# A decoder layer with gathered experts: ScalarE scales the third and fourth tile's convolution taps, and TensorE sums them earlier

## The chip, the cores and the metric

The kernel runs on one core of one Trainium2 chip. A core has five engines with instruction streams of their own: TensorE (PE in the profile; its weight loads are PEld), VectorE (DVE), ScalarE (ACT), GpSimd (POOL) and SyncE (SP). They meet only at semaphores. Each executes its stream in order, so an instruction that waits holds up everything behind it on its engine. The metric is the device time of one launch in microseconds; before the change it is 2165.56 us, the median of three runs.

## The reference, cut to what matters

One decoder layer is computed for a prompt of 512 tokens, in four tiles of 128, and for 32 sample tokens. Each tile has a front part (projections, causal depthwise convolution, attention over keys that an indexer selects, merge, norm) and an expert part, in which each token reads 128 rows of a table u and 128 rows of a table v, chosen by top-k.

```python
def conformer_conv(u, prev, conv_w, conv_b, ...):      # CONV_W = 31, D_CONV = 512
    full = jnp.concatenate([prev, u], axis=1)
    y = lax.conv_general_dilated(full, conv_w[:, None, :], ..., feature_group_count=D_CONV) + conv_b
    y = jax.nn.silu(layer_norm(y, conv_ln_g, conv_ln_b))
    ...

def attn_prompt(q, k, v, qi, ki, wi):                  # per block of 128 queries
    idx, valid = select_keys(indexer_scores(qib, wib, ki), pb, topk)      # topk = 128
    return sparse_attend(qb, _gather_rows(k, idx), _gather_rows(v, idx), valid)

def peer_ffn(x2, ...):
    u = peer_u[eidx]; v = peer_v[eidx]                 # 128 rows each for a token
    a = jax.nn.gelu(jnp.einsum('nd,nhed->nhe', x2, u), approximate=False)
    return jnp.einsum('nhe,nhed->nd', (g * a), v)
```

Per channel the convolution is a sum over 31 shifts ("taps") of the gated tokens, each scaled by one weight of the channel.

## The kernel before, in words

The prompt's tiles are counted t = 0 to 3. "Third tile" is t = 2 and "fourth tile" t = 3. Their fronts run while the expert part of the tile ahead (t = 1, t = 2) is under way on the same engines.

**Expert part.** GpSimd issues 544 gathers of u rows and 544 of v rows (line 884), each of 128 rows of 1,024 floats, into a ring of 11 places of the buffer `rings`. A u gather is used up by one "dot" of VectorE (line 2177, 128x1024). Two v gathers are used up by one "expert pair" of TensorE (line 1780, eight traced matmuls of 128x512), for which ScalarE copies a small column of weights (line 1262, 128x4) for each two pairs. A gather into a place waits until the row that lay there has been used (lines 877 to 880), so GpSimd can be at most a ring ahead of VectorE and TensorE.

**Front of the third and fourth tile.** After the load and the rotation, TensorE transposes the parts, ScalarE copies them to SBUF (line 987, the convolution's input `uT3` last). Then come, in this order: the index phase (for each of eight heads a product of TensorE, line 1526, a Relu of ScalarE, line 1132, and a weighted sum of VectorE into `score`, line 2076); the top-k of 16 rounds on VectorE (lines 1844 and 1847), in which the front needs neither TensorE nor ScalarE; and the attention of 16 heads (VectorE line 2037, ScalarE lines 1067 and 1082, TensorE lines 1613, 1596 and 1627).

**The taps.** Within the first part of the attention VectorE makes for each of the 31 taps one product of the shifted tokens with the tap's weights (`scaled_taps`, line 2022, 128x512), and TensorE adds it into the upper half of the bank `wide` by a matmul with the identity (`added_taps`, line 1513). Two buffers take turns: `stage_1`, and `score`, which is free once the top-k is over. So scaling tap k waits for the sum of tap k - 2, and the sum of tap k waits for its scaling. After tap 31 ScalarE moves the sum out of the bank (`convolved`, line 1018). The attention needs the bank's upper half only from its ninth head on (line 1621).

**What sets the order.** Each engine's stream is put together by a merge of generators (`run`, `merge`, lines 619 to 630). Each generator yields planned times before its pieces, and the piece with the least time is put next. A front's times are fractions (`AT_IDX` = 0.05, `AT_TOPK` = 0.09, `AT_ATT` = 0.20, `AT_TAIL` = 0.48) that `CLOCK_T` turns into planned microseconds for the third and fourth tile. `tap_at` gives the taps' times. The plan decides only the order in each stream; at run time semaphores decide.

## Time and profile before

| | |
|---|---|
| runs | 2162.22, 2165.56, 2166.86 us; median 2165.56 us |
| profiled execution | 2169.81 us; span of its instructions 2168.0 us |
| busy, share of the span | TensorE 66%, weight loads 25%, VectorE 62%, ScalarE 13%, GpSimd 56% |
| granted TensorE clock, mean | 0.823 |
| DMA, mean over the span | 315 GB/s |

The span is what lies between the first and the last instruction, and the shares are means over stages that differ much. Four stages concern the change. In the third tile's front the index phase runs from about 740 to 757 us, the top-k to 800 us, the taps to 855 us beside the attention's first heads, and the rest of the attention to 892 us. In the fourth tile's front these are 1136, 1152, 1195, 1259 and 1306 us. In the rows below an instruction stands with its line, its engine and the names of what it writes and reads; "idle before <-releaser" is how long its engine had waited for it and what ended that wait. A tap's matmul is traced as two instructions (x2), an expert pair as eight (x8).

### The profile page before, as it was taken

How to read it: one execution, taken by the hardware profiler on the slowest of the kernel's cores; microseconds unless marked ns; L12 is line 12 of the kernel's file. 1: busy time of each engine (PE TensorE's matmuls, PEld its weight loads, DVE VectorE, ACT ScalarE, POOL GpSimd, SP SyncE). 2: the span in 40 equal slices, each digit the busy share in tenths (PEclk: the TensorE clock that was granted, in tenths of full speed). 3: DMA queues.
4: the chain of work that ended last, by engine and by line, in shares of the span. 5: the costliest groups of instructions: out<-in, count | busy, mean ns of one | idle time of the engine just before them, and what ended most of it. 6: DMA issues, size and time to landing. Idle time of an engine off the chain costs nothing.

```text
span 2168.0 us, 18693 instructions
## 1 busy us (share of the span) xinstructions
PE 1435.1 (66%) x5765; PEld 541.4 (25%) x5765; DVE 1342.3 (62%) x3160; ACT 273.3 (13%) x667; POOL 1216.8 (56%) x1107
## 2 busy tenths in 40 slices
PE   7889999488964518776655887855533347566335
PEld 3444444232220104322111342311100012122001
DVE  4318965991159599947939876587569974103441
ACT  1411111112000202201010121200000002000000
POOL 1003454665555655856867567677656565346654
PEclk9999999799998859589676988887666567779878
DMA  8717999878888977989999789999989979979996
GB/s 303 315 63 258 324 366 373 300 242 312 301 309 307 389 254 251 340 277 331 332 387 351 236 316 352 351 355 336 373 277 397 360 258 362 354 282 336 375 348 245
DMA packets 207454, 682.68 MB, mean 315 GB/s; under 512 B 26901, under 2 KB 54933, under 8 KB 200787
## 3 DMA queue, kind: packets, MB, share of 16 engines
q0 software_dynamic: 157376, 581.67, 74.3%
q1 hardware_dynamic: 42971, 90.66, 11.6%
q10 hardware_dynamic: 7008, 9.17, 1.2%
q8 instruction: 46, 0.75, 0.1%
q14 instruction: 53, 0.43, 0.1%
HBM read 668.88 MB, written 12.94 MB: 314 GB/s over the span
## 4 chain that ended last, share of the span: by engine, by line
PE 34%; DVE 24%; issue 12%; POOL 11%; DMA 8%; SPq 5%; another core or an unknown queue 3%; ACT 2%; POOLq 0%; ACTq 0%; DVEq 0%
POOL rings L884 11%; DVE rings L2177 9%; PE acc L1780 7%; PE acc L1349 6%; DMA rings<-peer_v,late 4%; PE wide L1349 3%; PE wide L1374 3%; DVE small L1844 2%; PE bank L1487 2%; PE wide L1513 2%; SPq L740 2%; PE acc L1316 2%; DMA rings<-peer_u,late 2%; SPq L748 2%
## 5 line engine op out<-in xcount | busy, mean ns | idle before, releaser
L884 POOL DMA_INDIRECT rings<-peer_u,late x544 | 621.3, 1142 | 487.4 <-DVE late L2177 193.5
L1780 PE MATMUL acc<-rings,z_stages 128*32 128x512 f32 x2048 | 564.2, 711 | 426.9 <-issue 232.4
L884 POOL DMA_INDIRECT rings<-peer_v,late x544 | 587.0, 1079 | 362.3 <-PE acc L1780 160.3
L2177 DVE CUSTOM_DVE_ANT_0 rings<-rings,uah 128x1024 f32<-128x1024 f32 x288 | 347.3, 1223 | 150.4 <-DMA rings<-peer_u,late 142.6
L2177 DVE CUSTOM_DVE_ANT_0 rings<-rings,late 128x1024 f32<-128x1024 f32 x256 | 308.9, 1223 | 86.7 <-DMA rings<-peer_u,late 71.0
L1780 PEld LDWEIGHTS acc<-rings,z_stages 128*32 128x32 f32 x2048 | 120.6, 121 | 817.3 <-issue 811.5
L1349 PE MATMUL acc<-rings 128*128 128x512 f32 (+1 forms) x352 | 147.1, 569 | 0.1
L1513 PE MATMUL wide<-z_stages,ident_s 128*128 128x512 f32 x96 | 56.7, 675 | 90.9 <-DVE z_stages L2022 90.6
L1262 ACT COPY z_stages<-late 128x4 f32<-128x4 f32 x136 | 26.1, 199 | 547.3 <-PE acc L1780 416.0
L1349 PEld LDWEIGHTS acc<-rings 128*128 128x128 f32 x352 | 62.6, 190 | 70.1 <-issue 69.3
L1316 PE MATMUL acc<-rings 128*128 128x512 f32 (+2 forms) x176 | 70.1, 546 | 14.2 <-DMA small<-quarter 12.4
L1349 PE MATMUL wide<-rings,uah 128*128 128x512 f32 (+1 forms) x176 | 74.3, 565 | 1.3 <-DVE late L1894 1.3
L1941 DVE MAX8 uah<-zt 128x8 f32<-128x128 f32 x68 | 19.4, 285 | 84.5 <-ACT zt L1050 68.0
L1627 PE MATMUL wide<-keep,soft_score 128*128 128x64 f32 x320 | 50.2, 305 | 21.7 <-ACT soft_score L1082 17.8
L1374 PE MATMUL wide<-w_out_s,uah 128*128 128x512 f32 x128 | 63.5, 644 | 1.4 <-ACT uah L1028 1.4
L1067 ACT ACTIVATE soft_score<-soft_score,small 128x128 f32<-128x128 f32 (+3 forms) x64 | 35.7, 558 | 213.1 <-DVE small L2042 213.0
L1487 PE MATMUL bank<-w_query_s,uah 128*128 128x512 f32 x128 | 61.2, 620 | 1.4 <-ACT uah L1035 1.4
L1627 PEld LDWEIGHTS wide<-keep,soft_score 128*128 128x128 f32 x320 | 46.9, 218 | 49.4 <-ACT soft_score L1082 31.0
L1513 PE MATMUL wide<-soft_score,ident_s 128*128 128x512 f32 x90 | 51.6, 657 | 5.0 <-DVE soft_score L2022 5.0
L1596 PE MATMUL bank<-keep,queries 64*128 64x128 f32 (+3 forms) x128 | 48.4, 526 | 4.7 <-issue 4.7
L1513 PEld LDWEIGHTS wide<-z_stages,ident_s 128*128 128x128 f32 x96 | 16.6, 203 | 119.4 <-issue 96.5
L2177 DVE DVE_READ_ACCUMULATOR2_ANT late<- 128x1 f32 x544 | 44.7, 82 | 0.0
(296 smaller groups left out, 1592.9 us busy)
## 6 DMA issues: line engine op xcount, KB each, us to landing
rings<-w_in SPq DMA_DIRECT2D x36, 1024.0 KB, 7.1
rings<-peer_u,late POOLq DMA_INDIRECT x544
rings<-peer_v,late POOLq DMA_INDIRECT x544
z_rows<-z_stages ACTq DMA_DIRECT2D x30, 256.0 KB
soft_score<-ln SPq DMA_DIRECT2D x6, 1024.0 KB, 7.7
zt<-z_rows SPq DMA_DIRECT2D x2, 2596.0 KB
w_out_s<-w_out POOLq DMA_DIRECT2D x1, 4096.0 KB, 17.1
w_query_s<-w_query POOLq DMA_DIRECT2D x1, 4096.0 KB, 14.0
```

What stands on the lines that cost most here:

```text
L740: return sp.value_load(page_s[0:1, at:at + 1], min_val=0, max_val=N_POOL - 1)
L748: sp.dma_start(smp_ki[r][k // 2][rows, j * PAGE:(j + 1) * PAGE], io["kidx_T"][pages[j]]).then_inc(kidx_in[r], 16)
L884: nc.gpsimd.indirect_dma_start(ring[:, place, :], None, table, offs).then_inc(row_in[place], 16)
L1316: last = nc.tensor.matmul(acc[:, i % 2 * BLK + lo:i % 2 * BLK + hi], xT_0[:, k, :], w[:, c, :], start=(k == 0), stop=(k == KC - 1))
L1349: last = nc.tensor.matmul(z_bank[j][:, 0:width], x[j][:, m, :], w[:, c, :], **flags)
L1374: last = nc.tensor.matmul(dst[0:n, half * BLK:(half + 1) * BLK], lhs[:, c, 0:n], rhs[:, c, half * BLK:(half + 1) * BLK], start=(c == 0), s ...
L1487: last = nc.tensor.matmul(s_bank[r][0:n, :], aT3[:, c, 0:n], wqu[:, c, r * BLK:(r + 1) * BLK], start=(c == 0), stop=(c == KC - 1))
L1513: nc.tensor.matmul(wide[:, BLK:], ident[:, :], scaled_of[k % 2].rearrange("p c n -> p (c n)"), start=(k == 0), stop=(k == CONV_W - 1), ski ...
L1596: last = nc.tensor.matmul(s_bank[g % 2][:, k * seen:(k + 1) * seen], qT3[half_rows[h % 2], h // 2, :], kT3[half_rows[h % 2], h // (N_HEADS ...
L1627: last = nc.tensor.matmul(wide[:, o * HEAD_DIM:(o + 1) * HEAD_DIM], pt2[:, g % 2, at * P:(at + 1) * P], v3[:, j, kv * HEAD_DIM:(kv + 1) * ...
L1780: last = nc.tensor.matmul(acc_v[QUAD * j:QUAD * (j + 1), half * BLK:(half + 1) * BLK], lone[:, quad % LONE, j, QUAD - 1 - m:2 * QUAD - 1 - m],
L2177: V.tensor_tensor_reduce(out=ring[:, place, :], in0=ring[:, place, :], in1=h, scale=1.0, scalar=0.0, op0=ALU.mult, op1=ALU.add, accum_out= ...
```

## The change

For the third and fourth tile the scaling of the taps goes from VectorE to ScalarE: each tap is four activations (`Copy` with the tap's weight as a scale for each partition), one for each group of 128 channels, where VectorE made one product of 128x512. The taps' planned times go from fractions 0.204 to 0.33 to 0.047 to 0.21, that is from the attention's first part to the time from the transposes to the attention; TensorE's sums follow at +0.008. Since `score` is in use then, the second buffer is another part of `zt` (the gates of the convolution's input, used up by then). The second tile keeps VectorE, its buffers and its times; only the move out of the bank gets a planned time that is 0.007 later.

```diff
-    scaled_of = (stage_1.rearrange("p (c n) -> p c n", c=CC), score.rearrange("p (c n) -> p c n", c=CC))
+    by_channels = lambda x: x.rearrange("p (c n) -> p c n", c=CC)
+    scaled_1 = (by_channels(stage_1), by_channels(score))
+    scaled_later = (by_channels(stage_1), by_channels(zt[:, Z_B:Z_B + D_CONV]))
...
-    def tap_at(k):
+    def tap_at(t, k):
 
-        return AT_ATT + 0.004 + 0.126 * k / CONV_W
+        return AT_ATT + 0.004 + 0.126 * k / CONV_W if t == 1 else 0.047 + 0.163 * k / CONV_W
+
+    def scaled_of(t, k):
+
+        return (scaled_1 if t == 1 else scaled_later)[k % 2]
...
@@ ScalarE @@
+        def scaled_taps(t):
+
+            for k in range(CONV_W):
+                yield tap_at(t, k)
+                if k == 0:
+                    act.wait_ge(t_copied, groups_before(t) + GROUPS)
+                if taps_before(t) + k >= 2:
+                    act.wait_ge(tap_added, taps_before(t) + k - 1)
+                for c in range(CC):
+                    last = nc.scalar.activation(scaled_of(t, k)[:, c, :], uT3[:, c, k:k + P], ACT.Copy,
+                                                scale=cp[:, c, k:k + 1])
+                last.then_inc(tap_scaled, 1)
...
-                yield from merge(itertools.chain(rectified(t), attention(t, AT_ATT, AT_TAIL)), convolved(t))
+                yield from merge(itertools.chain(rectified(t), attention(t, AT_ATT, AT_TAIL)),
+                                 itertools.chain(scaled_taps(t) if t >= 2 else iter(()), convolved(t)))
...
@@ TensorE, added_taps @@
-                yield tap_at(k) + 0.003
+                yield tap_at(t, k) + (0.003 if t == 1 else 0.008)
...
@@ VectorE @@
-                yield from merge(attention(t, AT_ATT, AT_TAIL), scaled_taps(t))
+                yield from merge(attention(t, AT_ATT, AT_TAIL), scaled_taps(t) if t == 1 else iter(()))
```

What this does to the streams is seen at three places. The changed kernel's lines lie 20 further down in the parts of TensorE and VectorE (2177 becomes 2197, 1780 becomes 1800, 1513 becomes 1533).

VectorE, the start of the third tile's attention; L2022 is a scaled tap, L2177 a dot, L2037 with L2042 one head of the attention. Before:

```order
L2022 TENSOR_TENSOR z_stages<-uah,conv_p 128x512
L2177 ISA rings,late<-rings,uah 128x1024
L2177 ISA late 128x1
L2022 TENSOR_TENSOR soft_score<-uah,conv_p 128x512
L2037 ISA soft_score,small<-bank,soft_score 128x384
L2037 ISA small 128x1
L2042 TENSOR_SCALAR small<-small 128x1
L2022 TENSOR_TENSOR z_stages<-uah,conv_p 128x512
L2177 ISA rings,late<-rings,uah 128x1024
L2177 ISA late 128x1
L2022 TENSOR_TENSOR soft_score<-uah,conv_p 128x512
```

And now (L2197 is the dot, L2057 with L2062 the head):

```order
L2197 ISA rings,late<-rings,uah 128x1024
L2197 ISA late 128x1
L2057 ISA soft_score,small<-bank,soft_score 128x384
L2057 ISA small 128x1
L2062 TENSOR_SCALAR small<-small 128x1
L2197 ISA rings,late<-rings,uah 128x1024
L2197 ISA late 128x1
```

The 31 taps are gone from between the dots; the order of the dots and the heads is the same.

ScalarE, the fourth tile's index phase; L1132 is a head's Relu, L943 the copy of the values ahead of it. Before:

```order
L1112 COPY uah<-uah 128x4x30
L987 COPY uah<-bank 128x4x128
L943 COPY keep<-zt 128x256
L1132 ACTIVATE soft_score<-bank 128x512 x5
L1262 COPY z_stages<-late 128x4
L1132 ACTIVATE soft_score<-bank 128x512 x3
```

And now (L1152 is the Relu, L1027 a tap's four pieces):

```order
L949 COPY keep<-zt 128x256
L1027 ACTIVATE z_stages<-uah,conv_p 128x128 x4
L1152 ACTIVATE soft_score<-bank 128x512
L1027 ACTIVATE zt<-uah,conv_p 128x128 x4
L1152 ACTIVATE soft_score<-bank 128x512
L1027 ACTIVATE z_stages<-uah,conv_p 128x128 x4
L1152 ACTIVATE soft_score<-bank 128x512
L1027 ACTIVATE zt<-uah,conv_p 128x128 x4
L1152 ACTIVATE soft_score<-bank 128x512
L1027 ACTIVATE z_stages<-uah,conv_p 128x128 x4
```

A tap stands ahead of each Relu, the first one too.

TensorE, from the fourth tile's index products (L1526) over its first two score products (L1596) to the attention; L1780 are expert pairs, four for a pair, L1513 is a tap. Before:

```order
L1526 MATMUL bank<-keep,queries 128x512 x3
L1780 MATMUL acc<-rings,z_stages 32x512 x4
L1526 MATMUL bank<-keep,queries 128x512 x5
L1780 MATMUL acc<-rings,z_stages 32x512 x4
L1596 MATMUL bank<-keep,queries 128x512 x2
L1780 MATMUL acc<-rings,z_stages 32x512 x20
L1513 MATMUL wide<-z_stages,ident_s 128x512
L1513 MATMUL wide<-soft_score,ident_s 128x512
```

And now (L1546 index product, L1533 tap, L1800 expert pair):

```order
L1546 MATMUL bank<-keep,queries 128x512 x2
L1533 MATMUL wide<-z_stages,ident_s 128x512
L1546 MATMUL bank<-keep,queries 128x512
L1533 MATMUL wide<-zt,ident_s 128x512
L1800 MATMUL acc<-rings,z_stages 32x512 x4
L1546 MATMUL bank<-keep,queries 128x512
L1533 MATMUL wide<-z_stages,ident_s 128x512
L1546 MATMUL bank<-keep,queries 128x512
L1533 MATMUL wide<-zt,ident_s 128x512
L1546 MATMUL bank<-keep,queries 128x512
L1533 MATMUL wide<-z_stages,ident_s 128x512
L1546 MATMUL bank<-keep,queries 128x512
```

Six taps stand ahead of the last index product, the rest between the expert pairs of the top-k, four or five taps to a pair; the attention's heads have none.

## Rows read from the trace of the kernel before

**Rows 1.** The stages' view: busy us of each engine (instructions), granted clock, DMA share, GB/s

```profile
744.00:757.00 13.00, 7.70 (x30) 2.09 (x26) 7.15 (x13) 3.63 (x6) 9.58 (x10) 0.91 1.03 409
757.00:801.00 44.00, 0.00 (x0) 0.00 (x0) 42.83 (x93) 0.00 (x0) 21.76 (x20) 0.50 0.81 267
801.00:856.00 55.00, 46.07 (x144) 20.88 (x144) 54.52 (x111) 10.04 (x28) 30.55 (x26) 0.92 0.76 238
856.00:935.00 79.00, 57.36 (x155) 31.10 (x154) 71.13 (x134) 14.52 (x35) 65.23 (x46) 0.65 0.89 317
1136.00:1152.00 16.00, 13.15 (x32) 3.12 (x32) 15.15 (x23) 4.71 (x10) 12.76 (x11) 0.79 0.86 293
1152.00:1195.00 43.00, 17.46 (x40) 3.20 (x40) 41.84 (x83) 1.48 (x2) 30.12 (x28) 0.68 0.98 367
1195.00:1265.00 70.00, 61.94 (x219) 27.59 (x220) 57.34 (x113) 14.47 (x36) 41.90 (x33) 0.93 0.73 246
```

**Rows 2.** The chain of waits by line, 757 to 935 us

```profile
by line: POOL rings L884 31.6%; DVE rings L2177 29.0%; issue 12.2%; DVE soft_score L1847 5.3%; DVE small L1844 4.3%; DVE z_stages L2022 4.3%; DVE soft_score L2022 4.3%; DMA rings<-peer_u,late 3.6%; DVE soft_score L2037 2.2%; PE wide L1513 1
```

**Rows 3.** Waits of GpSimd, 801 to 856 us: total us, times, longest

```profile
POOL rings L884 <- DVE late L2177: 22.6, 21, 2.4
```

**Rows 4.** Timeline of GpSimd: start us, us, operation [idle before <-releaser]

```profile
801.25 0.94 POOL L884 DMA_INDIRECT rings<-peer_u,late  x1 [2.45 <-DVE late L2177]
...
856.06 1.68 POOL L884 DMA_INDIRECT rings<-peer_u,late  x1 [0.87 <-DVE late L2177]
...
887.99 0.95 POOL L884 DMA_INDIRECT rings<-peer_u,late  x1 [0.30 <-issue]
...
932.26 1.98 POOL L884 DMA_INDIRECT rings<-peer_u,late  x1 [0.30 <-issue]
```

**Rows 5.** Timeline of VectorE, third tile's first scaled tap and the dot behind it

```profile
805.00 0.69 DVE L2022 TENSOR_TENSOR z_stages<-uah,conv_p 128x512 f32<-128x512 f32 x1
805.60 1.22 DVE L2177 CUSTOM_DVE_ANT_0 rings<-rings,uah 128x1024 f32<-128x1024 f32 x1
```

**Rows 6.** The chain of waits by line, 1195 to 1265 us

```profile
by line: PE wide L1513 39.1%; PE acc L1780 13.1%; PE bank L1596 11.4%; DVE rings L2177 10.0%; PE wide L1627 6.4%; PE bank L1613 5.4%; DVE soft_score L2037 3.7%; issue 3.6%; DVE z_stages L2022 2.7%; ACT queries L1018 1.3%; ACT soft_score L10
```

**Rows 7.** Waits of GpSimd, 1195 to 1265 us

```profile
POOL rings L884 <- PE acc L1780: 19.7, 5, 6.4
```

**Rows 8.** Timeline of GpSimd, fourth tile's taps

```profile
1195.22 1.68 POOL L884 DMA_INDIRECT rings<-peer_v,late  x1 [2.51 <-DVE late L2177]
...
1206.44 1.63 POOL L884 DMA_INDIRECT rings<-peer_u,late  x1 [0.30 <-issue]
1214.51 0.94 POOL L884 DMA_INDIRECT rings<-peer_u,late  x1 [6.44 <-PE acc L1780]
...
1264.23 0.94 POOL L884 DMA_INDIRECT rings<-peer_u,late  x1 [2.47 <-PE acc L1780]
```

**Rows 9.** Timeline of TensorE: index product, expert pair, taps, expert pair

```profile
1136.51 1.12 PE L1526 MATMUL bank<-keep,queries 64*128 64x512 f32 x2 [0.79 <-ACT soft_score L1132]
...
1188.71 3.34 PE L1780 MATMUL acc<-rings,z_stages 128*32 128x512 f32 x8 [4.07 <-DMA rings<-peer_v,late]
1199.94 2.04 PE L1513 MATMUL wide<-z_stages,ident_s 128*128 128x512 f32 x2 [7.88 <-DVE z_stages L2022]
...
1212.33 1.91 PE L1780 MATMUL acc<-rings,z_stages 128*32 128x512 f32 x8
```

**Rows 10.** The chain of waits in order of time: start us, us, what

```profile
1222.93 1.91 PE wide L1513 x4
```

**Rows 11.** ScalarE's groups by form, from SBUF with a pointer bias

```profile
L1067 ACT ACTIVATE soft_score<-soft_score,small 128x128 f32<-128x128 f32 x16 | 6.2, 390 | 4.0 <-DVE small L2042 4.0
```

**Rows 12.** The chain of waits in order of time, a gather's landing

```profile
928.25 6.39 DMA rings<-peer_u,late
```

**Rows 13.** Timeline of VectorE, fourth tile's index sums

```profile
1136.57 0.75 DVE L2076 SCALAR_TENSOR_TENSOR soft_score<-soft_score,small,conv_acc 128x512 f32<-128x512 f32 x1 [5.57 <-ACT soft_score L1132]
...
1148.17 1.56 DVE L2076 SCALAR_TENSOR_TENSOR soft_score<-soft_score,small 128x512 f32<-128x512 f32 x2
```

More of the change, by code:

```diff
@@ L1010, in conv @@
             last.then_inc(conv_act, 1)
+        def scaled_taps(t):
[9 more added lines that the diff above has]
+                last.then_inc(tap_scaled, 1)
         def convolved(t):
-            yield tap_at(CONV_W) + 0.005
+            yield tap_at(t, CONV_W) + 0.012
             act.wait_ge(tap_added, taps_before(t + 1))
@@ L1512, in added_taps @@
                 pe.wait_ge(tap_scaled, taps_before(t) + k + 1)
-                nc.tensor.matmul(wide[:, BLK:], ident[:, :], scaled_of[k % 2].rearrange("p c n -> p (c n)"),
+                nc.tensor.matmul(wide[:, BLK:], ident[:, :], scaled_of(t, k).rearrange("p c n -> p (c n)"),
                                  start=(k == 0), stop=(k == CONV_W - 1), skip_group_check=True).then_inc(tap_added, 1)
@@ L2014, in scaled_taps @@
             for k in range(CONV_W):
-                yield tap_at(k)
+                yield tap_at(t, k)
                 if k == 0:
@@ L2021, in scaled_taps @@
                     dve.wait_ge(tap_added, taps_before(t) + k - 1)
-                V.tensor_tensor(scaled_of[k % 2], uT3[:, :, k:k + P], cp[:, :, k:k + 1].to_broadcast([P, CC, P]),
+                V.tensor_tensor(scaled_of(t, k), uT3[:, :, k:k + P], cp[:, :, k:k + 1].to_broadcast([P, CC, P]),
                                 ALU.mult).then_inc(tap_scaled, 1)
```

## The prediction, made before the changed kernel ran

> **What bounds the kernel now.** I read the stages' view first, then the chain of waits in the two stretches that the change touches, then what GpSimd waits for there, and last the timelines of single instructions. The gathers are the bulk of the work, and where they slow down is where the kernel loses time. The stages' view shows two such stretches, and they are the two in which the taps lie: 801 to 856 us moves 238 GB/s and 1195 to 1265 us moves 246 GB/s, against 317 GB/s and 367 GB/s in the stretches beside them [rows 1].
>
> In the third tile VectorE is the limit. It is busy 54.52 of 55 us [rows 1], the chain from 757 to 935 us runs over VectorE's dots and taps first and over GpSimd's issues behind them [rows 2], and GpSimd waits 22.6 us for dots [rows 3]. From 856.06 us on GpSimd waits for nothing but its own issue. The timeline of GpSimd, read through, has 27 intervals between gathers from 801.25 to 856.06 us (one record is missing), 17 to 887.99 us and 27 to 932.26 us [rows 4]: 2.03, 1.88 and 1.64 us each. The middle pace belongs to a VectorE that eats up the landed rows without a pause, the last one to a VectorE that waits for rows.
>
> In the fourth tile the limit is TensorE. Its taps hold 39.1% of the chain from 1195 to 1265 us [rows 6], it is busy 61.94 of 70 us [rows 1], and GpSimd waits 19.7 us for expert pairs that stand behind taps [rows 7]: the gather after 1206.44 us starts at 1214.51 us, when the pair of 1212.33 us has run [rows 8, 9]. There are 32 intervals from 1195.22 to 1264.23 us, 2.16 us each.
>
> **What the change takes away, third tile.** VectorE loses 31 taps. One is 0.69 us long but takes 0.60 us of the stream (805.00 to 805.60 us) [rows 5], so 31 x 0.60 = 18.8 us, all in a stretch where VectorE is full. Behind it stands GpSimd, which can't give all of that back. Without taps VectorE still has a stock of landed rows, which took from 856 to 888 us to run down; so I let 18 gathers go at 1.88 us and the other 53 of the 71 at 1.64 us: 34 + 87 = 121 us where 131.0 us stand now [rows 4]. That is -10 us. The bounds are 0 (all 71 at 1.88 us would be 133 us) and -18.8 us (all of VectorE's time comes back).
>
> **Fourth tile.** TensorE's 31 taps leave the stretch; a tap takes 0.96 us of it at the high clock (x4, two taps, 1.91 us) [rows 10], 29.6 us in all. The 32 gathers then go at 1.64 us: 52.5 instead of 69.0 us [rows 8], -16.5 us. Bounds: at 1.88 us it is 60 us, -9 us; at the rate of the top-k before it, 367 GB/s for 246 x 70 = 17.2 MB [rows 1], it is 47 us, -22 us.
>
> **What it adds: ScalarE.** The trace has no scaling from SBUF by a pointer in pieces of 128. The nearest row is an Exp from SBUF with a pointer bias, 390 ns [rows 11]. Four pieces take 1.56 us without overlap and 1.29 us with the 0.09 us by which VectorE's tap and the dot behind it overlap [rows 5]; with an overlap of 0.15 us, my lower bound, it is 1.1 us. I take 1.25 us, 39 us for a tile. From 1136 to 1195 us ScalarE is busy 4.71 + 1.48 us of 59 [rows 1], so this fits. What it costs is order. A tap stands ahead of the first Relu of the index phase, and behind that Relu are the sum on VectorE, the top-k and the dots in the same stream: +1.3 us in each tile.
>
> The Trainium skill has a rule that speaks against this part. "VectorE: DVE Perf Modes", section on the TRN2 errata, says that a ScalarE or VectorE instruction which reads SBUF pays a fixed extra latency each time, so that one wide operation is cheaper than four narrow ones; "ScalarE: Activation LUTs", What ACT_TABLE_LOAD costs, gives 186 ns + 0.833 ns an element, 93 ns more for a pointer and 93 ns of overlap, from which I estimate 1.27 us for the four pieces against VectorE's one at 0.60 us. By it ScalarE spends twice what VectorE saves, and the sum stays, since ScalarE has the room. The 390 ns of a 128-wide piece agree with it.
>
> **What it adds: TensorE in the index phase and the top-k.** From the third tile's index phase to its attention TensorE is idle 5.3 of 13 us and then 44 of 44 us [rows 1], so its taps are covered; I add 1 us for the taps between the index products, 2.3 with the tap ahead, say +2 us. In the fourth tile six taps (5.8 us) stand ahead of the last index product, and TensorE had 16 - 13.15 = 2.9 us idle there [rows 1]: +3 us, with the tap ahead +4 us. The sums of VectorE that wait for it took from 1136.57 to 1149.7 us [rows 13]. Bounds: 0, and all 5.8 us at the low clock with its tap twice as long, +12 us.
>
> From there to 1195 us TensorE has to fit eight index products and two score products at 1.1 us (the pair of rows of one is 1.12 us), seven expert pairs at 1.9 us and 31 taps at 0.96 us [rows 9, 10]: 11 + 13 + 30 = 54 of 59 us. It fits, at the high clock only, and pairs that wait for a row hold the taps behind them. The streams show four or five taps between two pairs. I take +3 us for pairs that come late at the end of the top-k. Tap 31 on ScalarE stands behind the first Exp of the attention, which waits for the end of the top-k; TensorE's sum of it stands ahead of the first head's transposes: +1 us for both tiles.
>
> **The sum.** -10 - 16.5 + 2 + 4 + 3 + 1 = -16.5 us. Nothing later is tied to an absolute time: the fourth tile's front starts when the third tile is routed, the sample's when the fourth is. Against the profiled execution (2169.81 us, its span 2168.0 us and 1.8 us around it) that is 2153.3 us. The runs' median is 4.2 us under the profiled execution, so I predict 2149 us for the median.
>
> **Rivals.**
> - *Both stretches free up wholly.* VectorE's 18.8 us and GpSimd's 19.7 us of waits [rows 7] both come back and the additions are 6 us: -32 us, 2133 us. For it: in the top-k of the fourth tile the DMA reaches 367 GB/s beside a VectorE busy 41.84 of 43 us [rows 1], so gathers can go faster than my 1.64 us. Against it: 1.88 us with VectorE full of dots [rows 4].
> - *GpSimd is the limit anyway.* The gathers keep 1.88 us while VectorE is dense: third tile 0, fourth tile -9 us, additions +10 us: 2166 us, no change. For it: issues of up to 1.98 us with no wait [rows 4].
> - *TensorE runs the taps at the low clock, slower.* The place is the fourth tile from the index phase to the top-k's end. In it the granted clock was 0.79 and 0.68, and in the third tile's top-k 0.50 [rows 1]; a tap's two rows at 1199.94 us, after an idle time of 7.88 us, took 2.04 us, and a pair 3.34 us against 1.91 us [rows 9]. At the low level (1.2 GHz) 31 x 1.9 + 7 x 3.3 + 10 x 2.2 = 104 us have to go into 59 us; if half the time is low, the last pairs come some 20 us late, and a ring of 11 gathers at 1.5 us (28 in 43 us of the top-k), less 6.4 us of landing [rows 1, 12], covers about 10 us. It decides once TensorE falls behind by more than that. Then the fourth tile's gain turns into waits of GpSimd in the top-k: -10 + 2 - 16.5 + 12 + 22 = +9.5 us, 2175 us. Against it: in the fourth tile's taps, with TensorE almost full, the granted clock was 0.93 [rows 1], and here it would be as full. The Trainium skill states the ground of both, in "TensorE: Matmul & The Clock Gate", section on the HAM clock gate: the clock is throttled by default and activity releases it. The rows at 1199.94 us and 1222.93 us agree.
> - *The taps are scaled by ScalarE but still end in the attention*, since the two buffers tie ScalarE to TensorE and TensorE waits for rows. Then TensorE keeps part of its taps behind 1195 us; half of the fourth tile's gain goes: 2157 us. It lies within the forecast's own range.
>
> **How the numbers follow.** Forecast, with its smaller relatives (2141 to 2159 us): 0.50. Both stretches free: 0.16. GpSimd the limit: 0.18. Low clock: 0.16. A measurement of this kernel can tell about 0.2%, 4.3 us, from no change. Faster by more than that: 0.48 of the forecast, 0.16, and 0.04 of GpSimd's case, 0.68. Within it: 0.02, 0.12 and 0.02, 0.16. Slower: 0.02 and 0.14, 0.16. The range goes from the free case's lower side to just above no change, 2130 to 2170 us; it leaves out most of the low clock's case.
>
> **What would show it.** VectorE from the end of the third tile's top-k: heads of the attention and dots with nothing between them, and soon waits for landed rows. GpSimd's waits for dots (22.6 us) and for pairs (19.7 us) shrink to a few us. The 71 and 32 intervals average 1.7 us. ScalarE's 124 pieces for a tile at about 0.39 us. The index phase 2 and 4 us longer. The prediction is wrong if the fourth tile's top-k stretch falls under 340 GB/s with GpSimd waiting for pairs in it, or if GpSimd's intervals stay at 1.9 us without a wait.

## The result, and the profile after

The changed kernel took 2141.7 us (median of 9 runs, 2136.9 to 2159.6), the kernel before beside it 2168.6 us (9 runs). The ratio is 0.9884, 95% interval 0.9843 to 0.9924: faster by 16 to 34 us. Predicted were 2149 us, 2130 to 2170. The profiled execution's span is 2139.7 us, 28.3 us under the one before.

The stages' view after, for the third tile's index phase, top-k and attention, then the same of the fourth:

```profile
core 0: us, PE busy (x) PEld busy (x) DVE busy (x) ACT busy (x) POOL busy (x), PEclk, DMA share, GB/s
741.00:760.00 19.00, 17.25 (x43) 4.99 (x44) 7.94 (x14) 11.25 (x36) 7.87 (x10) 0.91 0.89 326
760.00:803.00 43.00, 26.27 (x50) 7.03 (x48) 41.90 (x89) 28.22 (x89) 22.03 (x21) 0.89 0.78 248
803.00:885.00 82.00, 59.89 (x178) 36.88 (x178) 73.38 (x156) 20.75 (x57) 65.32 (x46) 0.50 0.84 285
1124.00:1140.00 16.00, 15.92 (x40) 4.30 (x40) 12.88 (x20) 12.60 (x37) 10.05 (x9) 1.00 0.94 335
1140.00:1183.00 43.00, 36.32 (x90) 9.84 (x88) 41.87 (x82) 27.78 (x91) 28.84 (x28) 0.92 0.86 317
1183.00:1286.00 103.00, 76.67 (x313) 35.69 (x308) 66.33 (x138) 26.79 (x63) 71.70 (x63) 0.80 0.88 314
```

TensorE and ScalarE are now busy in both top-k stretches, in which TensorE idled in the third tile and ScalarE all but idled in both [rows 1], and VectorE has room in the third tile's attention (busy 73 of 82 us). What GpSimd waits for in the third and in the fourth attention (columns: total, times, longest):

```profile
POOL rings L890 <- issue: 13.1, 43, 0.3
POOL rings L890 <- DVE late L2197: 4.8, 3, 2.4
```

```profile
POOL rings L890 <- issue: 18.3, 60, 0.3
POOL rings L890 <- PE acc L1800: 10.8, 2, 8.8
POOL rings L890 <- DVE late L2197: 2.5, 1, 2.5
```

The 22.6 us for dots [rows 3] are 4.8 now; the 19.7 us for pairs [rows 7] are 10.8, of which 8.8 are one stall (below). The windows here are whole attentions and so longer than those of the rows before, which makes the comparison a cautious one. The timeline of GpSimd, the gathers that answer to [rows 4] and [rows 8]:

```profile
805.76 0.94 POOL L890 DMA_INDIRECT rings<-peer_u,late  x1 [2.44 <-DVE late L2197]
807.57 1.68 POOL L890 DMA_INDIRECT rings<-peer_u,late  x1 [0.87 <-DVE late L2197]
809.55 1.99 POOL L890 DMA_INDIRECT rings<-peer_u,late  x1 [0.30 <-issue]
811.85 1.50 POOL L890 DMA_INDIRECT rings<-peer_u,late  x1 [0.30 <-issue]
...
836.45 0.94 POOL L890 DMA_INDIRECT rings<-peer_u,late  x1 [0.30 <-issue]
...
923.40 1.99 POOL L890 DMA_INDIRECT rings<-peer_u,late  x1 [0.30 <-issue]
...
1185.85 1.68 POOL L890 DMA_INDIRECT rings<-peer_v,late  x1 [2.52 <-DVE late L2197]
1187.83 1.64 POOL L890 DMA_INDIRECT rings<-peer_u,late  x1 [0.30 <-issue]
...
1236.68 0.94 POOL L890 DMA_INDIRECT rings<-peer_u,late  x1 [2.03 <-PE acc L1800]
```

Gathers can be counted (here from 0; each profile has all 1,088), so the same piece of work can be timed in every profile. The 312th gather (the first after the third tile's top-k) to the 382nd are 70 intervals: 131.0 us before (801.25 to 932.26 us), 117.6 us after. The prediction counted 71, taking one record for missing; none is (there are 26 intervals up to 856.06 us, 2.11 us each, and not 27). From the 541st (the first after the fourth tile's top-k) to the 573rd are 32 intervals: 69.0 us before, 50.8 us after. The whole of the 28.3 us in terms of gathers: up to the 312th +4.5 us, to the 382nd -13.4, to the 541st -0.5, to the 573rd -18.2, to the end -0.7. The fourth tile's index phase, 2.6 us longer, lies in the stretch with the -0.5: what stands ahead of it, from the third tile's last row write on, took 200.8 us before and 197.6 us after, and 194.7 to 199.8 us in the other profiles, so a few us of the profile's 28.3 are owed to the one profile of before.

ScalarE's taps in the third tile's top-k (start, length of the four pieces):

```profile
770.49 1.26 ACT L1027 ACTIVATE z_stages<-uah,conv_p 128x128 f32<-128x128 f32 x4
771.80 1.28 ACT L1027 ACTIVATE zt<-uah,conv_p 128x128 f32<-128x128 f32 x4
```

### The profile page after: what moved, and what is told of

Same layout as the page of the kernel before. It is cut to its first block, busy times and chain, and to the rows that moved or that the text cites. A ratio compares the mean times of both kernels' runs of the same rounds, so it can differ in the third digit from the quotient of the medians.

```text
span 2139.7 us, 18879 instructions
## 1 busy us (share of the span) xinstructions
PE 1453.3 (68%) x5765; PEld 545.7 (26%) x5765; DVE 1306.5 (61%) x3098; ACT 347.3 (16%) x915; POOL 1208.7 (56%) x1107
## 4 chain that ended last, share of the span: by engine, by line
PE 35%; DVE 23%; POOL 13%; issue 11%; DMA 9%; SPq 5%; ACT 2%; another core or an unknown queue 1%; POOLq 0%; ACTq 0%; DVEq 0%
POOL rings L890 13%; DVE rings L2197 8%; PE acc L1800 8%; DMA rings<-peer_v,late 6%; PE acc L1369 6%; PE wide L1394 4%; PE wide L1369 3%; DVE small L1864 3%; PE bank L1507 2%; SPq L746 2%; PE acc L1336 2%; DVE uah L1867 2%; SPq L754 2%; DVE soft_score L1867 1%; DVE conv_acc L2027 1%
## 5 line engine op out<-in xcount | busy, mean ns | idle before, releaser
L1800 PE MATMUL acc<-rings,z_stages 128*32 128x512 f32 x2048 | 565.2, 713 | 405.8 <-DMA rings<-peer_v,late 220.2
L2197 DVE CUSTOM_DVE_ANT_0 rings<-rings,uah 128x1024 f32<-128x1024 f32 x288 | 347.3, 1224 | 155.7 <-DMA rings<-peer_u,late 138.8
L2197 DVE CUSTOM_DVE_ANT_0 rings<-rings,late 128x1024 f32<-128x1024 f32 x256 | 308.6, 1223 | 89.0 <-DMA rings<-peer_u,late 79.7
L1800 PEld LDWEIGHTS acc<-rings,z_stages 128*32 128x32 f32 x2048 | 120.6, 122 | 792.9 <-issue 787.8
L1533 PE MATMUL wide<-z_stages,ident_s 128*128 128x512 f32 x96 | 56.8, 676 | 58.9 <-DVE z_stages L2042 32.1
L1647 PE MATMUL wide<-keep,soft_score 128*128 128x64 f32 x320 | 59.1, 341 | 37.4 <-ACT soft_score L1101 32.8
L1369 PEld LDWEIGHTS acc<-rings 128*128 128x128 f32 x352 | 62.6, 190 | 70.0 <-issue 69.5
L1647 PEld LDWEIGHTS wide<-keep,soft_score 128*128 128x128 f32 x320 | 52.7, 246 | 74.7 <-ACT soft_score L1101 56.1
L1616 PE MATMUL bank<-keep,queries 64*128 64x128 f32 (+3 forms) x128 | 54.6, 567 | 0.0
L2057 DVE CUSTOM_DVE_ANT_0 soft_score<-bank,soft_score 128x128 f32<-128x128 f32 (+3 forms) x64 | 29.7, 487 | 29.1 <-PE bank L1616 23.2
L2197 DVE DVE_READ_ACCUMULATOR2_ANT late<- 128x1 f32 x544 | 44.5, 82 | 0.0
L1336 PEld LDWEIGHTS acc<-rings 128*128 128x128 f32 x176 | 32.4, 195 | 44.5 <-issue 27.3
```

Of the source, the lines that this page charges most:

```text
L1336: last = nc.tensor.matmul(acc[:, i % 2 * BLK + lo:i % 2 * BLK + hi], xT_0[:, k, :], w[:, c, :], start=(k == 0), stop=(k == KC - 1))
L1369: last = nc.tensor.matmul(z_bank[j][:, 0:width], x[j][:, m, :], w[:, c, :], **flags)
L1533: nc.tensor.matmul(wide[:, BLK:], ident[:, :], scaled_of(t, k).rearrange("p c n -> p (c n)"), start=(k == 0), stop=(k == CONV_W - 1), skip ...
L1616: last = nc.tensor.matmul(s_bank[g % 2][:, k * seen:(k + 1) * seen], qT3[half_rows[h % 2], h // 2, :], kT3[half_rows[h % 2], h // (N_HEADS ...
L1647: last = nc.tensor.matmul(wide[:, o * HEAD_DIM:(o + 1) * HEAD_DIM], pt2[:, g % 2, at * P:(at + 1) * P], v3[:, j, kv * HEAD_DIM:(kv + 1) * ...
L1800: last = nc.tensor.matmul(acc_v[QUAD * j:QUAD * (j + 1), half * BLK:(half + 1) * BLK], lone[:, quad % LONE, j, QUAD - 1 - m:2 * QUAD - 1 - m],
```

## Experiments

Twelve runs were made, each with the kernel before beside it. The kernels with an edit take the taps' engine and times from a table with one entry for each tile: `TAPS_BY` is V for VectorE and A for ScalarE; `TAPS_AT` has the fraction at which the first tap is planned, the fractions that 31 taps span, and how much later TensorE's sum and ScalarE's move out of the bank are planned. The changed kernel is 'A' with (0.047, 0.163, 0.008, 0.012) for tiles 2 and 3, before is 'V' with (0.204, 0.126, 0.003, 0.005); tile 1 has the latter in all of them, but for its last number, which is 0.012 in the changed kernel. Lines that start with + are the tables as they ran. The expectations call it the two-limits theory that VectorE holds the third tile's attention and TensorE the fourth's. Chips differ: before took 2165.6 us on the chip of the first four, 2119 to 2120 us on those of the others (the part behind the fourth tile is some 40 us shorter there). So times are compared as ratios, and pieces of the trace only where a chip's speed doesn't show in them. This table is worked out from the timelines of all profiles, in us. "Index" is the first to the last sum of the index phase on VectorE, "top-k" from there to the bias behind it, "attention" from there to the reciprocal at its end; g3 is the 312th to the 382nd gather, g4 the 541st to the 573rd, counted from 0.

```
                 third tile                    fourth tile
                 index top-k attention  g3     index top-k attention  g4    ratio to before
before           15.1  43.6   93.4    131.0    12.4  43.4  113.9     69.0
after            19.1  43.6   81.9    117.6    15.0  43.4  103.2     50.8   0.9884
third_only       17.4  43.6   84.6    121.3    12.4  43.4  114.9     69.4   0.9992
fourth_only      16.3  43.6   93.1    128.8    18.1  43.5  100.0     51.1   0.9943
act_late         18.6  43.6   96.0    133.3    12.4  43.4  128.2     79.4   1.0068
dve_early        18.3  55.0   84.0    119.2    16.7  55.8   99.0     54.5   1.0039
 (the chips on which before took 2119 to 2120 us)
after_repeat     17.0  43.5   82.2    116.8    14.9  43.5   97.9     51.2   0.9897
after_index      12.7  43.6   81.3    116.8    12.4  43.4   99.2     51.9   0.9868
one_tap          13.5  43.7   81.6    116.0    12.4  43.4   99.2     49.4   0.9873
mix              12.7  43.6   78.3    113.1    22.0  43.3   98.5     50.2   0.9885
both_behind      12.6  43.7   82.6    121.0    12.4  43.4   99.2     50.5   0.9874
third_behind     12.6  43.6   79.7    114.2    12.4  43.4  116.5     69.1   0.9951
fourth_behind    12.7  43.6   94.0    129.2    12.4  43.4   96.0     51.1   0.9903
third_again      16.9  43.6   82.3    120.0    12.4  43.4  115.4     69.2   0.9976
```

How far a single profile can be trusted is seen where kernels plan a tile alike: third_behind, mix and both_behind have the same third tile and show 114.2, 113.1 and 121.0 us for g3; after, after_repeat, third_only and third_again have 116.8 to 121.3 us. So differences of a few us in g3 say nothing. g4 is steadier, 49.4 to 51.9 us in eight profiles.

**1. third_only.** The fourth tile's taps stay with VectorE, at their old place:

```diff
+    TAPS_BY = {1: 'V', 2: 'A', 3: 'V'}
+    TAPS_AT = {1: (0.204, 0.126, 0.003, 0.005), 2: (0.047, 0.163, 0.008, 0.012), 3: (0.204, 0.126, 0.003, 0.005)}
```

> The third tile's taps are scaled by ScalarE from the transposes on, as in the changed kernel; the fourth tile's are left as they were. Two-limits theory: the third tile gains VectorE's 18.8 us less what GpSimd can't give back and less a later index phase. In the changed kernel the stretch between the start of the third tile's index phase and the last write of its rows was 6.4 us shorter; this kernel shows the same -6 to -7 us there, and the fourth tile's attention still has its 19.7 us of waits for pairs: about -6 us in all (ratio 0.997). Rival, the two tiles help each other (the third tile's earlier end is lost in the fourth unless that is changed too): the end within 2 us of before. Rival, the gain is VectorE's alone: -15 us or more here.

2162.2 us, ratio 0.9992 (0.9956 to 1.0028). In the table the third tile's attention loses 9 us and the fourth tile stays as before, as the two-limits theory has it, but the time shows next to none of it. The expected -6 us and no gain at all both lie in the interval; -15 us, the gain from VectorE alone, does not. Left open here, taken up in 9 and 10.

**2. fourth_only.** The same with the tiles exchanged: ScalarE for `t == 3`, the third tile as before.

> The fourth tile's taps are scaled by ScalarE from the transposes on; the third tile's are left as they were. Two-limits theory: TensorE's taps leave the attention, GpSimd's 19.7 us of waits for pairs go, less 3 to 6 us for a later index phase and late pairs: -13 us between the fourth tile's indices and the last write of its rows, 2155 us (ratio 0.994), index phase 2.5 us longer, attention about 10 us shorter than before's. Rival, the gain comes from VectorE: here it would be about as large as in the third tile alone. Rival, half of the gain comes from elsewhere (the parts outside the changed places, 5.6 us shorter in the changed kernel): this kernel and the third tile's would sum to less than 20 us.

2151.9 us, ratio 0.9943 (0.9914 to 0.9972), -12 us. g4 is 51.1 us, attention 14 us shorter, index phase 5.7 us longer (2.5 expected). Of these 5.7 us some 3 are TensorE's clock: from 1133 to 1141 us it had mostly the low level (granted clock 0.57 in this row), and a pair took 3.63 us there instead of 1.91 us.

```profile
1133.00:1141.00 8.00, 8.00 (x15) 1.70 (x14) 5.74 (x9) 4.42 (x14) 3.80 (x5) 0.57 0.97 378
```

The rival on VectorE falls: here the gain is larger than in the third tile alone. The last rival does not fall: the two kernels sum to some 14 us, under the 20 us that it names. Their errors of 6 to 8 us each can't tell this from the 25 us of the changed kernel, and 9 to 12 ask again.

**3. act_late.** ScalarE scales, at the old times:

```diff
+    TAPS_BY = {1: 'V', 2: 'A', 3: 'A'}
+    TAPS_AT = {1: (0.204, 0.126, 0.003, 0.005), 2: (0.204, 0.126, 0.008, 0.012), 3: (0.204, 0.126, 0.008, 0.012)}
```

> ScalarE scales the taps of the third and fourth tile, but at the places of before, between the heads of the attention: the engine changes, the time does not. Two-limits theory: the third tile has VectorE free and TensorE with room, so it keeps most of its gain, -6 to -10 us, less what ScalarE's 1.2 us a tap puts ahead of each Exp and copy; the fourth tile stays bound by TensorE (taps and products of 62 of 70 us), so its stretch keeps its 19 us of waits for pairs and gains nothing or loses some us: total -3 to -9 us, 2160 us. Rival, VectorE's relief is all: most of the 25 us is there. Rival, ScalarE in the attention holds up the heads, and both tiles get slower: +5 us or more.

2179.6 us, ratio 1.0068 (1.0038 to 1.0099), slower. My theory falls and the last rival holds: the third tile keeps nothing of VectorE's relief (g3 133.3 us), the fourth loses 10 us in g4. The third and the fourth tile's attention, and what VectorE waits for in the third's:

```profile
804.00:900.00 96.00, 73.05 (x238) 38.13 (x238) 72.40 (x158) 57.22 (x177) 63.88 (x46) 0.82 0.75 245
1196.00:1324.00 128.00, 100.49 (x367) 43.99 (x366) 65.86 (x139) 61.84 (x182) 76.10 (x63) 0.86 0.74 256
```

```profile
DVE soft_score L2062 <- PE bank L1621: 22.9, 7, 4.7
```

VectorE is busy 72 of 96 us, no longer full, and waits 22.9 us for the score products of the heads. These stand on TensorE behind a tap, the tap behind ScalarE's four pieces, and dots stand behind the head on VectorE. GpSimd still waits 20.5 us for dots there. So an engine with room isn't enough: left between the heads, the taps take back all that VectorE was relieved of. The kernel puts two things into the heads' way, ScalarE's pieces (new) and TensorE's sums (there before, but now behind ScalarE); which of them costs more was not separated.

**4. dve_early.** VectorE scales, at the new times and with the new second buffer (the scaling is merged with the index sums and the top-k of VectorE's stream; ScalarE has none).

> VectorE scales the taps of the third and fourth tile as before, but at the new times, from the transposes to the attention (with the new second buffer): the time changes, the engine does not. Two-limits theory: in the fourth tile TensorE is relieved in the attention, but VectorE, busy 41.84 of 43 us in the top-k, gets 18.8 us more there: the top-k becomes some 15 us longer, of which the attention gives back 16: about 0 for the fourth tile. In the third tile VectorE is full at both places: 0 within 3 us. Total 0, -5 to +8 us. Rival, TensorE's time is all that counts: the fourth tile keeps its -13 us, and the total is -13 us or better. Rival, GpSimd sets the pace in the top-k and VectorE's 18.8 us are hidden there: also -13 us; the waits of GpSimd for dots in the top-k tell it (they grow by 10 us or more by my theory, by under 5 by the rival).

2171.2 us, ratio 1.0039 (1.0005 to 1.0074), as expected. The two top-k stretches, in which VectorE is full, grow by 11.4 and 12.4 us, the index phases by 3.2 and 4.3; the attentions give back 9.4 and 15:

```profile
758.00:813.00 55.00, 37.52 (x44) 9.50 (x42) 53.87 (x109) 0.55 (x1) 22.64 (x21) 0.56 0.67 204
1152.00:1208.00 56.00, 39.90 (x78) 9.30 (x76) 54.09 (x102) 1.48 (x2) 31.11 (x27) 0.79 0.70 235
```

The sign that was to decide, GpSimd's waits for dots in the top-k, came in the third tile only, 32.7 us where before has 18.5 us. In the fourth there are none; there GpSimd waited for pairs instead, which it did not before:

```profile
POOL rings L895 <- DVE late L2206: 32.7, 20, 2.1
POOL rings L895 <- PE acc L1805: 13.0, 4, 4.8
```

By 3 and 4 neither half of the change gains anything alone: the time has to be another (out of the attention) and the engine has to be another (VectorE is full in the top-k too).

**5. after_repeat.** The changed kernel again, as the base of the next three.

> The changed kernel again, beside the next three: the base they are compared with. Ratio 0.988 within its interval. Theory: in the third tile, from the first index sum to the end of the attention 145 us where before had 152 us; in the fourth 162 where before had 170 us. Rival (the parts outside the changed places, which were 5.6 us shorter in the one profile): the stretch from the last row write of the fourth tile to the end is again near 807 us; by the theory it lies anywhere between 806 and 826 us, as in the kernels so far, and has nothing to do with the change.

2098.2 us beside 2120.5 us, ratio 0.9897 (0.9868 to 0.9927). First index sum to attention's end: 142.7 and 156.3 us, 2 and 6 us less than expected. The end, from the fourth tile's last row write on, took 774.8 us; on another kind of chip this can't be held against the 807 us.

**6. after_index.** The taps start behind the index phase:

```diff
+    TAPS_BY = {1: 'V', 2: 'A', 3: 'A'}
+    TAPS_AT = {1: (0.204, 0.126, 0.003, 0.005), 2: (0.091, 0.119, 0.008, 0.012), 3: (0.091, 0.119, 0.008, 0.012)}
```

> As the changed kernel, but the taps of both tiles start behind the index phase (31 taps from 0.091 to 0.21 of the tile's plan instead of 0.047 to 0.21). Theory that the taps between the index products cost the index phase 3 us (third) and 3 us (fourth): the index phases go back to about 15 and 12.5 us. Third tile: 31 x 1.2 = 37 us of ScalarE fit the 43 us of the top-k, so -3 us. Fourth tile: TensorE has then 46 of 43 us in the top-k, the taps end 6 to 10 us into the attention, and pairs come later: +3 to +8 us. Total 0 to +5 us against the changed kernel. Rival, the index phase is lengthened by pairs in TensorE's stream and not by the taps: no change in the index phases, total +5 to +10 us.

2091.1 us, ratio 0.9868 (0.9841 to 0.9896), beside 0.9897 for the changed kernel; the intervals overlap. The index phases are 4.3 and 2.5 us shorter: they were the taps' price. The expected loss in the fourth tile isn't there (g4 51.9 us): the last tap is summed at 1171.4 us, 8 us into the attention, but pairs are hardly late (GpSimd waited 1.7 us for them in the top-k and 2.8 us in the attention), and the top-k keeps its pace:

```profile
1120.00:1163.00 43.00, 37.59 (x92) 10.56 (x90) 41.91 (x81) 31.73 (x105) 31.72 (x30) 0.98 0.98 364
```

**7. one_tap.**

```diff
-            for k in range(CONV_W):
+            for k in range(N_TAPS[t]):
...
+    N_TAPS = {1: 31, 2: 1, 3: 1}
```

It leaves out 30 of the 31 taps of the third and the fourth tile, so what it computes is another convolution; the engines and the times are the changed kernel's.

> As the changed kernel with 1 of the 31 taps in the third and the fourth tile; the other 30 are left out, so the output is another. It is the ceiling of what moving the taps can bring. Theory (two limits, and a price of 3 us for each index phase and some us for late pairs in the fourth top-k): 7 to 12 us under the changed kernel, 2130 us; attention stretches as in the changed kernel within 2 us, since there GpSimd's own pace and the landed rows set them. Rival, GpSimd's pace in the attention is slowed by the taps' traffic still: also the attentions become shorter. Rival, the moved taps are wholly hidden: within 3 us of the changed kernel.

2092.7 us, ratio 0.9873 (0.9849 to 0.9896). With 60 of 62 taps gone the kernel is 5.5 us by medians below the changed one, between the theory's 7 to 12 us and the rival's 3 us, with intervals that overlap, and level with after_index. So within some 4 us the moved taps are hidden in the top-k, and what they still cost was in the index phases (here 13.5 and 12.4 us).

**8. mix.** The third tile's taps behind the index phase, the fourth's at the transposes but closer together:

```diff
+    TAPS_AT = {1: (0.204, 0.126, 0.003, 0.005), 2: (0.091, 0.112, 0.004, 0.012), 3: (0.047, 0.148, 0.006, 0.03)}
```

> The third tile's taps start behind its index phase (0.091 to 0.203), the fourth's stay at the transposes but are planned closer together (0.047 to 0.195), so that in both tiles the last tap stands ahead of the attention's first Exp on ScalarE and its first transposes on TensorE. Theory: third tile -3 us for the index phase and -1 us for the last tap; fourth tile -1 us for the last tap, pairs 0 to 2 us later: -3 to -5 us against the changed kernel. Rival, the index phase's price is not the taps': within 1 us of the changed kernel.

2092.8 us, ratio 0.9885 (0.9859 to 0.9911), beside 0.9897: 3 to 5 us under the changed kernel as expected, but the intervals overlap. Third tile as expected or better (g3 113.1 us). The fourth's index phase took 22.0 us instead of 14.9. The timeline of TensorE there (L1538 a tap, L1551 a product; kernels with an edit have these lines 5 higher):

```profile
1105.98 2.05 PE L1538 MATMUL wide<-z_stages,ident_s 128*128 128x512 f32 x2 [1.57 <-ACT z_stages L1032]
1107.96 2.07 PE L1551 MATMUL bank<-keep,queries 64*128 64x512 f32 x2
1109.96 2.08 PE L1538 MATMUL wide<-zt,ident_s 128*128 128x512 f32 x2
...
1116.90 1.13 PE L1538 MATMUL wide<-z_stages,ident_s 128*128 128x512 f32 x2
1117.95 1.12 PE L1551 MATMUL bank<-keep,queries 64*128 64x512 f32 x2
```

With a tap between two products a head costs 2.1 us at the high clock and 4.0 us at the low one; with no tap there the sums follow each other every 12.4 / 7 = 1.8 us. From 1106 to 1117 us the granted clock was 0.54, from 1117 to 1128 us 1.00. Some 5 of the 7 us are this low stretch (four taps and products at 2.0 us instead of 1.05, a pair at 2.9 us instead of 1.8); the other 2 are the closer plan, by which one more tap and one more product stand between the first tap and the last product. It is the low-clock rival of the prediction, in the index phase instead of the top-k. It isn't this plan's own: fourth_only had it for 7 us, the two profiles of the changed kernel not at all.

**9. third_behind.** Only the third tile is changed, as in mix; the fourth is as before the change:

```diff
+    TAPS_BY = {1: 'V', 2: 'A', 3: 'V'}
+    TAPS_AT = {1: (0.204, 0.126, 0.003, 0.005), 2: (0.091, 0.112, 0.004, 0.012), 3: (0.204, 0.126, 0.003, 0.005)}
```

> Of the kernel before this one only the third tile's part; the fourth tile's taps as in the kernel before the change. Theory (gains of the two tiles add up, and the 0.9992 of the first one-tile kernel was a third tile that paid 3 to 4 us in its index phase, within its own error of the -6 us expected): -14 to -17 us, ratio 0.993. Rival (a third tile that ends earlier gains nothing by the end, since the fourth waits for something else): ratio 0.998 or more, with the fourth tile longer by what the third was shorter.

2108.7 us beside 2118.8 us, ratio 0.9951 (0.9928 to 0.9974): -10 us. Less than its profile promises (g3 and the whole third tile are 15 us shorter than in kernel 11's) and less than the -14 to -17 us expected, but the rival falls: the ratio is under its 0.998, and the fourth tile isn't longer than before's.

**10. third_again.** The kernel of 1 once more.

> The first one-tile kernel again (third tile's taps from the transposes on, fourth tile as before): its profile had the third tile 10 us shorter than before's, its ratio was 0.9992, 0.9956 to 1.0028. Theory: attention of the third tile 82 to 85 us instead of 93, index phase 1 to 4 us longer; -6 to -9 us by the end, ratio 0.996 to 0.997. Rival, the one-tile change at this place really gives nothing by the end: ratio 0.999 again, with the fourth tile (219 us from its first index sum to its last row write before) or the part behind it longer by 6 us or more.

2117.2 us beside 2119.9 us, ratio 0.9976 (0.9953 to 1.0000). Neither value is excluded. The two runs together put this one-tile change at 0 to -8 us, while the third tile is 8 to 10 us shorter in its profiles up to its last row write. Some of it seems to be lost later; where, one profile of each can't tell, since the part behind the fourth tile varies by 13 us between profiles of one kind of chip (769 to 782 us).

**11. fourth_behind.** Only the fourth tile is changed, as in after_index:

```diff
+    TAPS_BY = {1: 'V', 2: 'V', 3: 'A'}
+    TAPS_AT = {1: (0.204, 0.126, 0.003, 0.005), 2: (0.204, 0.126, 0.003, 0.005), 3: (0.091, 0.119, 0.008, 0.012)}
```

> Only the fourth tile's part; the third tile's taps as before the change. Theory: TensorE out of the attention, nothing paid in the index phase (12.4 us): fourth tile from the first index sum to the last write of its rows 202 us, where before had 219 us, -15 to -17 us, ratio 0.9925; with the third tile's part it adds up to the kernel with both within 4 us. Rival: the fourth tile's gain hangs on the third's: ratio 0.996 or more, and the sum of the two kernels falls short of the one with both by 6 us or more.

2098.7 us, ratio 0.9903 (0.9879 to 0.9928): -20.6 us, more than expected. The waits of GpSimd in the attention:

```profile
POOL rings L895 <- issue: 18.3, 60, 0.3
POOL rings L895 <- DVE late L2202: 2.1, 1, 2.1
POOL rings L895 <- PE acc L1805: 0.3, 1, 0.3
```

Of before's 19.7 us for pairs 0.3 are left, and the third tile keeps its waits (24.3 us for dots). This half alone makes most of the gain.

**12. both_behind.** 9 and 11 together.

> Taps of both tiles behind the index phase, the third tile's planned to end ahead of the attention (0.091 to 0.203), the fourth's at 0.091 to 0.21. It joins the better halves of the two kernels before. Theory, from their profiles: third tile from the first index sum to the end of the attention 135 us (before 152), fourth 155 (before 170); -29 to -33 us against before, ratio 0.985 to 0.987. Rival: what the third tile wins comes back as waits in the fourth or behind it: ratio no better than 0.990, as the changed kernel.

2095.5 us, ratio 0.9874 (0.9846 to 0.9901), -27 us and at the lesser end of what was expected. The two halves sum to -1.46%, both together give -1.26%: 4 us apart, equal within the intervals. It isn't better than after_index or one_tap: three kernels without a price in the index phase lie at 0.9868 to 0.9874, the changed kernel at 0.9884 and 0.9897. That the earlier taps cost the changed kernel time is shown in the profiles (4.3 and 2.5 us in the index phases), and in the times only as a tendency of 2 to 6 us.

## Why the prediction was right

*The third tile's stretch.* Forecast -10 us (18 gathers at 1.88 us, the rest at 1.64); with 70 intervals instead of 71 its own paces give -12 us. Measured: 18 gathers took 34.8 us (forecast 33.8), all 70 117.6 us, 1.68 us each; -13.4 us. The two ends of the range, 0 and -18.8 us, were GpSimd's limit and VectorE's whole time; it lies between, as argued. That VectorE was the limit is read from the profiles: GpSimd's waits for dots fell from 22.6 to 4.8 us, and VectorE now waits for landed rows. No run relieves VectorE alone, since whatever moves the scaling moves TensorE's sums too or, as experiment 3, puts ScalarE between the heads. That experiment showed a condition that the prediction didn't have: the relief comes to nothing while the taps stay between the heads.

*The fourth tile's stretch.* Forecast -16.5 us (32 gathers in 52.5 us), measured -18.2 us (50.8), and 49.4 to 51.9 us in every kernel with at most a few taps in this attention, dve_early's 54.5 apart. This is nearer to all of the 19.7 us of waits than the forecast had it. That it is TensorE's: fourth_behind lets the waits for pairs go, and act_late, in which VectorE is relieved as much, raises them to 32.2 us.

*ScalarE.* Taken 1.25 us a tap; 1.26 to 1.28 us measured for four pieces, 31 taps in 39 us where nothing holds them up (mix, third tile). By the Trainium skill's figures ("ScalarE: Activation LUTs", What ACT_TABLE_LOAD costs) four pieces are estimated at 1.26 us (the prediction has 1.27), and the trace agrees.

*What it adds.* Here the sum was off. Index phases +2 and +4 us forecast; +4.0 and +2.6 measured, and by after_repeat against after_index 4.3 and 2.5. The prediction took the third tile's taps for covered; in fact TensorE ran with hardly a pause in both index phases (17.25 of 19 us, 15.92 of 16 us). (Of the third's, chance may hold some: on the first chip, with no tap in it, it took 15.1, 16.3 and 18.6 us.) Late pairs at the end of the fourth top-k, +3 us forecast: there are late pairs (GpSimd waited 6.7 us for them, 317 GB/s instead of 367 [rows 1]), but they cost nothing, since the 541st gather waits 2.5 us for a dot behind the top-k on VectorE in both kernels [rows 8], and that top-k takes 43.4 us either way. By its own test (top-k stretch under 340 GB/s with waits for pairs) the prediction would have been wrong; the test was wrong, since it took late pairs for lost time. The rival in which TensorE's taps end in the attention came true only in name: 2 of 31 did in the fourth tile. The last tap, +1 us: the three profiles in which it stands ahead of the first Exp have a third attention of 78.3, 79.7 and 82.6 us, the others 81.3 to 84.6 us; not told apart. So by the gathers 3 of the 10 us of added cost were there, and the two gains were 5 us larger than forecast; this is the 12 us between the -16.5 and the -28 of the profile. In the runs it is -27 us, and -22 us on the second chip: the forecast's 16.5 fall 10 and 6 us short. The places and the engines were right, the sizes were not: nearly all the errors pointed the same way, and that the time lay 7 us and not 10 under the forecast's 2149 is luck, since before was 3 us slower beside the changed kernel than in the runs that the forecast started from.

*The rivals.* Both stretches wholly free (-32 us) came nearer in size than the forecast on the first chip (-27 us) and not on the second (-22 us). In kind it holds for the fourth tile (18.2 of 19.7 us came back) and not for the third, where GpSimd's own pace holds the gain at 13 of 18.8 us. GpSimd the limit anyway falls (1.68 and 1.59 us for a gather, not 1.88), though its mechanism is seen from 809 to 836 us in the third tile, 2.07 us a gather with no wait. The low clock didn't come in the top-k (granted clock 0.92, fourth tile). It came in the index phases of mix and fourth_only, for some 5 and 3 us.

## What to carry to other kernels

Look at the place in the order, not only for the engine that is full: work moved to an idle engine but left between two steps of a chain (a tap ahead of a head) still delays that chain. Move such work to a stretch whose length another engine sets, as VectorE's top-k does here, and start it behind a short phase in which three engines pass a piece from one to the next (here worth 4.3 and 2.5 us in the profiles). Count a unit of work, such as gathers, and time the same piece in each profile, before believing a difference of ends, and take the same stream's profile more than once: here g3 alone varies by up to 8 us.

## What was unexpected of the hardware

In the profile after, TensorE, ScalarE and VectorE all stood still from about 1248 to 1254 us, while the DMA engines went on at 410 GB/s. TensorE waited for ScalarE's copy, which started again at 1253.86 us; of ScalarE and VectorE the profile names nothing that it shows as having released them (`remote`):

```profile
1244.54 1.12 PE L1616 MATMUL bank<-keep,queries 64*128 64x512 f32 x2
1254.50 1.97 PE L1647 MATMUL wide<-keep,soft_score 128*128 128x64 f32 x8 [8.84 <-ACT soft_score L1101]
```

```profile
1253.86 0.58 ACT L1101 COPY soft_score<-bank 128x512 f32<-128x512 f32 x1 [8.17 <-remote]
```

```profile
1246.00:1254.00 8.00, 0.00 (x0) 0.00 (x0) 2.19 (x4) 0.14 (x1) 4.32 (x5) 0.57 1.02 410
```

It cost this profile about 5 us (attention 103.2 us, 96.0 to 100.0 us in the eight others with the fourth tile's taps moved); what it did to the runs isn't known. Its cause wasn't tried.

In the third tile's attention the granted clock was 0.75 to 0.82 with the taps in it (fourth_behind, act_late) and 0.50, the low level, in the changed kernel without them, with TensorE busy 60 of 82 us. No cost is seen: GpSimd waits for no pair there. In the fourth tile's attention it is 0.80 without taps and 0.86 in act_late.

GpSimd's issues take in turn 1.99 and 1.50 us from 809 to 834 us and 0.93 to 1.99 us, often 0.94, from 836 us on in the same stream, with no wait between them. In the slow part VectorE is busy 29.75 of 30 us, as this row shows, and 40.8 of 49 us behind it; in before the same turns come from 866 to 886 us, with VectorE busy 19.8 of 20 us. Whether it is VectorE that slows them wasn't tried.

```profile
806.00:836.00 30.00, 26.00 (x73) 15.36 (x73) 29.75 (x66) 9.35 (x28) 25.16 (x15) 0.50 0.75 232
```
